# Sliding-window layer of a four-layer decoder step: the prompt's attention and the samples' attention put into one phase

## What is computed

```python
SWA_GROUPS = ((128, 1), (512, 4), (2048, 16))     # window and dilation, 4 heads each, head size 64
q, k, v = jnp.split(h @ w_qkv, 3, axis=-1)        # q and k are then normalised per head
# prompt: every query sees the last win/dil keys at distance dil
s = einsum('bcnihd,bcnjhd->bcnhij', qb, kk) * HEAD_DIM ** -0.5 + bias   # masked outside the window
# samples: past rows come from cache_swa_kv0/1/2 (128, 512, 1024 rows kept), new rows are appended
s = einsum('bthd,btnhd->bthn', q, kg) * HEAD_DIM ** -0.5 + bias_tab[rel_bucket(n * dil)].T
lse = logsumexp(s); p = exp(s - lse); o = einsum('bthn,btnhd->bthd', p, vg)
# the three groups are weighted by the softmax of their lse, then  o @ w_out
# outputs too: the new caches (old rows shifted, new rows stored at the end)
```

## Time and profile before

| | |
|---|---|
| median of 3 runs | 2106.91 us (2106.85 to 2110.78) |
| profiled execution, its own time | 2107.75 us |
| its span, first to last instruction | 2106.1 us |
| TensorE matmul busy | 1934.6 us, 92% |
| VectorE, ScalarE, GpSimd busy | 1186.1, 960.5, 478.6 us |
| mean granted TensorE clock | 0.953 |

### The profile page before, as it was taken

How to read it: one execution, slowest core, us unless ns; L and a number is a source line. 1 busy time by engine, 2 the same in 40 slices (tenths; PEclk the granted TensorE clock), 3 DMA queues, 4 the chain that set the end, 5 groups by cost and what they waited for, 6 DMA issues and landing times. The chain is left out here.

```text
span 2106.1 us, 37643 instructions
## 1 busy us (share of the span) xinstructions
PE 1934.6 (92%) x14726; PEld 1830.9 (87%) x14726; DVE 1186.1 (56%) x2046; ACT 960.5 (46%) x1566; POOL 478.6 (23%) x480
## 2 busy tenths in 40 slices
PE   6899979999998678999997887999998999799999
PEld 4899969999997457999996666999988999699998
DVE  4677764555443235554445775555466777555543
ACT  3666663444342124443343554444347666434432
POOL 3222212333100002442102321333112222023420
PEclk9999989999998688999999998999999999899999
DMA  6367755555552094655656742665563667456554
GB/s 181 98 203 235 235 173 161 160 163 147 172 170 79 17 275 122 169 161 144 176 192 206 288 170 76 176 169 152 164 191 113 221 218 222 135 154 166 161 150 133
DMA packets 502033, 352.63 MB, mean 167 GB/s; under 512 B 14154, under 2 KB 487100, under 8 KB 501084
## 3 DMA queue, kind: packets, MB, share of 16 engines
q1 hardware_dynamic: 495156, 306.03, 49.9%
q0 software_dynamic: 6272, 43.92, 5.5%
q10 hardware_dynamic: 430, 0.29, 0.1%
HBM read 326.58 MB, written 50.63 MB: 179 GB/s over the span
## 5 line engine op out<-in xcount | busy, mean ns | idle before, releaser
L268 PE MATMUL ps<-xh,whi 128*128 128x288 f32 x2368 | 657.8, 304 | 10.0 <-PEq L176 9.9
L268 PE MATMUL ps<-xl,whi 128*128 128x288 f32 x2368 | 647.1, 300 | 0.0
L240 DVE TENSOR_TENSOR wlo<-raw,whi 128x2048 fp32r<-128x2048 f32 (+3 forms) x241 | 501.8, 2083 | 245.2 <-ACT whi L229 245.0
L229 ACT ACTIVATE whi<-raw 128x2048 fp32r<-128x2048 f32 (+3 forms) x241 | 419.1, 1740 | 263.5 <-PE ps L276 231.4
L268 PEld LDWEIGHTS ps<-xh,whi 128*128 128x128 f32 x2368 | 454.7, 192 | 12.2 <-issue 10.5
L268 PEld LDWEIGHTS ps<-xl,whi 128*128 128x128 f32 x2368 | 455.4, 192 | 0.8
L276 PE MATMUL ps<-xh,wlo 128*128 128x288 f32 x2368 | 354.6, 300 | 0.0
L276 PEld LDWEIGHTS ps<-xh,wlo 128*128 128x128 f32 x2368 | 328.8, 190 | 1.1
L520 POOL TENSOR_TENSOR gh<-sg,ut 128x288 f32<-128x288 f32 x88 | 216.3, 2458 | 353.0 <-ACT sg L461 353.0
L268 PE MATMUL ps<-hh,whi 128*128 128x288 f32 x704 | 189.7, 296 | 0.0
L268 PE MATMUL ps<-hl,whi 128*128 128x288 f32 x704 | 189.6, 297 | 0.0
(11 more groups left out here) (319 smaller groups left out, 2702.4 us busy)
## 6 DMA issues: line engine op xcount, KB each, us to landing
raw<-in_ffn_w_in SPq DMA_DIRECT2D x176, 512.0 KB, 5.0
raw<-in_ssm_w_in SPq DMA_DIRECT2D x80, 512.0 KB, 4.8
raw<-in_ffn_w_out SPq DMA_DIRECT2D x64, 384.0 KB, 4.0
raw<-in_ffn_w_out SPq DMA_DIRECT2D x64, 320.0 KB, 3.2
H<-in_state_ssm SPq DMA_DIRECT2D x32, 512.0 KB, 7.6
out_ssm_sample<-H SPq DMA_DIRECT2D x32, 512.0 KB, 6.5
raw<-in_ssm_w_out SPq DMA_DIRECT2D x32, 512.0 KB, 5.0
Kp_L<-in_cache_diff_k SPq DMA_DIRECT2D x64, 256.0 KB, 4.5
```

The lines of the kernel that those rows point to most:

```text
L229: act.activation(wts["hi"][:, s, 0:width], raw[:, s, 0:width], ACT.Copy).then_inc(hi_ready.sem, 1)
L240: dve.tensor_tensor(wts["lo"][:, s, 0:width], raw[:, s, 0:width], wts["hi"][:, s, 0:width].bitcast(F32), ALU.subtract).then_inc(lo_ready.s ...
L268: pe.matmul(out, W[0][:, kk, j, :], x_[:, k, :], stop=False, start=(part == 0 and kk == 0 and x_ is seg.hi), skip_group_check=True)
```

## The change

It removes the phase boundary inside layer 1's attention and writes the eight prompt units between the samples' instructions, on every engine. In words:

- `load_keys` is passed to `project`: the first round's keys (16 loads) go out on SyncE's queue in two halves, during and after the weight blocks. The wait on the page table moves into layer 2's own function.
- Keys are turned in two parts: 8 pieces of the wide cache (4 transposes each), then 8 pieces of the other two caches (3 transposes each), into one buffer `KT` that both parts use. Scores are made after each part.
- The second round's keys load into the same buffers as they come free; its values wait for the end of the first round's values (`pv_done`), since `V1`, `V0`, `V2` are used by both rounds.
- Turned pieces go round three PSUM banks, prompt scores have a place of their own (banks 3 and 4), the samples' scores and values share banks 5 and 6, the prompt's results are in bank 7.
- The prompt's bias and maximum are one VectorE instruction (`tensor_tensor_reduce`) instead of two.
- The new rows' 29 stores go out on GpSimd's queue instead of SyncE's. Behind them GpSimd copies the new keys' bias (`new_bias`), which the samples' maximum waits for.

```diff
-                        sp.wait_ge(table_in.sem, table_in.at(1))
...
+        def load_keys(sp, half):
+            for j in (2 * half, 2 * half + 1):
+                load_wide(sp, j, 0, K1[:, j, :, :], key_in[j])
+                load_rest(sp, j, 0, K0[:, j, :], K2[:, j, :, :], key_in[j])
...
-                Linear(4, 6, 2, columns(A["swa_w_out"][0], 6, 2)))
+                Linear(4, 6, 2, columns(A["swa_w_out"][0], 6, 2)), load_keys=load_keys)
...
+                for t in range(T):
+                    sp.dma_start(rb[32 * t:32 * t + 32, :], A["rel_bias"]).then_inc(loaded.sem, loaded.inc())
+                sp.dma_start(barred, A["barred_swa"]).then_inc(loaded.sem, loaded.inc())
+                sp.dma_start(oh, A["onehot_swa"]).then_inc(loaded.sem, loaded.inc())
...
+                for j in range(J):
+                    load_wide(sp, j, 1, V1[:, j, :, :], val_in)
+                    load_rest(sp, j, 1, V0[:, j, :], V2[:, j, :, :], val_in)
+                for j in range(J):
+                    sp.wait_ge(piece_turned.sem, piece_turned.at(at["key", 0, 2 * j + 1] + 1))
+                    load_wide(sp, J + j, 0, K1[:, j, :, :], key_in[j])
...
+                sp.wait_ge(pv_done.sem, pv_done.at(1))
+                for j in range(J):
+                    load_wide(sp, J + j, 1, V1[:, j, :, :], val_in)
+                    load_rest(sp, J + j, 1, V0[:, j, :], V2[:, j, :, :], val_in)
+                sp.wait_ge(copied.sem, copied.at(29))
...
-                        sp.dma_start(out[rows], KV[:, t, :, cols]).then_inc(stored.sem, stored.inc())
+                        pool.dma_start(out[rows], KV[:, t, :, cols]).then_inc(copied.sem, copied.inc())
...
+                for q in range(R):
+                    pool.wait_ge(laid.sem, laid.at(9 + NB))
+                    if q:
+                        pool.wait_ge(mx_ready.sem, mx_ready.at(q))
+                    pool.tensor_copy(bias[:, N_OLD:], BN[:, q, :]).then_inc(new_bias.sem, new_bias.inc())
...
+                unit_scores(0)
+                turn(0, 0, 0, 3)
+                unit_scores(1)
+                turn(0, 0, 3, 6)
+                tables_()
+                unit_scores(2)
+                turn(0, 0, 6, 8)
+                unit_turn(0)
+                scores_wide(0)
+                unit_values(0)
...
+                values(0)
+                unit_turn(5)
+                unit_values(5)
+                unit_scores(7)
+                scores_wide(1)
+                turn(1, 1, 0, 8)
+                scores_rest(1)
+                turn_out(0)
+                unit_turn(6)
+                unit_values(6)
+                unit_turn(7)
+                unit_values(7)
+                turn_probs(1)
+                values(1)
+                turn_out(1)
...
+                    dve.tensor_tensor_reduce(
+                        Su[:, r, :, 0:n], flat[:, 3 * 512:3 * 512 + 768].rearrange("p (g n) -> p g n", g=3)[:, :, 0:n],
+                        BT.rearrange("p h t k -> p h (t k)")[:, hh::4, 2 * P - n:2 * P], -1.0, 3.0e38,
+                        ALU.add, ALU.min, su[:, r, 0:1]).then_inc(u_lowest.sem, u_lowest.inc())
...
+                unit_lowest(0)
+                keys(0, 0, 0, 3)
+                lay_queries()
+                lay_tables()
+                unit_lowest(1)
+                unit_scale(0)
```

More of the change, by code:

```diff
@@ L1963, in swa @@
[L1963 to L1983 removed]
+            R = 2
@@ L2104, in swa @@
             at = {piece: n for n, piece in enumerate(order)}
-            mover = [0 if kind == "prob" and p == 0 else 1 if kind != "key" else p % 2 for kind, _, p in order]
+            mover = [0 if kind == "turned" else 1 if kind == "out" else p % 2 for kind, _, p in order]
             count = [sum(e == mover[n] for e in mover[:n + 1]) for n in range(len(order))]
-            def last_piece(j):
-                return (2 * N_OLD * (j + 1) - 1) // 512
             def wait_moved(eng, *piece):
@@ L2145, in _ @@
[L2145 to L2147 removed]
+                        val_in.sem, val_in.inc())
+                for j in range(J):
[4 more added lines that the diff above has]
+                    load_wide(sp, J + j, 0, K1[:, j, :, :], key_in[j])
@@ new lines, in tables_ @@
+                def tables_():
+                    pe.wait_ge(laid.sem, laid.at(8))
+                    pe.wait_ge(loaded.sem, loaded.at(T + 2))
+                    for g, lo, n in KEYS + tuple((g, N_OLD + g * T, T) for g in range(3)):
+                        out = ps[:, 7, lo - N_OLD:lo - N_OLD + n] if lo >= N_OLD else flat[:, 2560 + lo:2560 + lo + n]
+                        pe.matmul(out, LT[:, g, :], oh[:, lo:lo + n], start=True, stop=False)
+                        mm = pe.matmul(out, barred[:, N_OLD + 12:], barred[:, lo:lo + n], start=False, stop=True)
+                    mm.then_inc(tables.sem, tables.inc())
@@ L2230, in _ @@
-                pe.wait_ge(laid.sem, laid.at(4))
-                pe.wait_ge(loaded.sem, loaded.at(T + 2))
-                for g, lo, n in KEYS + tuple((g, N_OLD + g * T, T) for g in range(3)):
-                    new = lo >= N_OLD
-                    out = ps[:, 6, lo - N_OLD:lo - N_OLD + n] if new else flat[:, 2048 + lo:2048 + lo + n]
-                    pe.matmul(out, LT[:, g, :], oh[:, lo:lo + n], start=True, stop=False)
-                    mm = pe.matmul(out, barred[:, N_OLD + 12:], barred[:, lo:lo + n], start=False, stop=True)
@@ new lines, in unit_turn @@
+                def unit_turn(u):
+                    qt, hh, n, rows, r = unit(u)
+                    pe.wait_ge(u_summed.sem, u_summed.at(2 * u + 2))
+                    tiles = [(g, kt) for g in range(3) for kt in range(qt + 1)]
+                    for p in range(qt + 1):
+                        m = at["turned", u, p]
+                        wait_moved(pe, *order[m - 3])
+                        for k, (g, kt) in enumerate(tiles[3 * p:3 * p + 3]):
+                            mm = pe.matmul(ps[:, m % 3, k * P:(k + 1) * P], Su[:, r, g, kt * P:(kt + 1) * P], DR[:, r, :],
+                                           start=True, stop=True)
+                        mm.then_inc(piece_turned.sem, piece_turned.inc())
@@ new lines, in keys, with unit_exp @@
+                def keys(q, part, lo, hi):
+                    for i in range(lo, hi):
+                        if i % 2 == 0:
+                            move(act, copy, "key", q, 8 * part + i)
+                def unit_exp(u):
+                    qt, hh, n, rows, r = unit(u)
+                    act.wait_ge(u_lowest.sem, u_lowest.at(u + 1))
+                    act.activation(Su[:, r, :, 0:n], Su[:, r, :, 0:n], ACT.Exp, scale=-1.0, bias=su[:, r, 0:1],
+                                   accum_out=su[:, r, 1:2]).then_inc(u_weighed.sem, u_weighed.inc())
@@ L2293, in _ @@
+                unit_move(4)
+                unit_exp(5)
+                keys(1, 0, 4, 8)
+                move(act, copy, "prob", 0, 0)
+                unit_exp(6)
+                unit_move(5)
+                unit_exp(7)
+                keys(1, 1, 0, 8)
+                unit_move(6)
+                exp_sample(1)
+                unit_move(7)
+                move(act, copy, "prob", 1, 0)
             @block.vector
@@ L2371, in swa @@
+                unit_out(5)
+                unit_lowest(7)
+                unit_scale(6)
+                keys(1, 1, 0, 8)
+                lowest_of(1)
+                out(0)
+                unit_scale(7)
+                unit_out(6)
+                unit_out(7)
+                move(dve, copy, "prob", 1, 1)
+                stage_out(1)
+                out(1)
+        memB.close()
         mem.close()
```

595 lines of the change are left out of this document (293 added, 302 removed).

## The result

The changed kernel takes 2059.51 us (median of four runs, 2056.42 to 2063.7); the kernel before takes 2108.85 beside it (2106.85 to 2113.36). The ratio is 0.9761, with a 95% interval of 0.9736 to 0.9785: faster by 2.4%. The profiled execution of the changed kernel has a time of 2056.42 us, a span of 2054.8 and a mean granted clock of 0.971.

A forecast was written before the change was run, and what follows sets the result against it. Bound: layer 1 attention's serial chain at the low clock. Terms 6.6 + 10.9 + 1.5 + 56.0 + 11.4 = 86.4 us against 135.8, 49.4 less: 2107.75 - 49.4 = 2058.4, forecast 2058 us, range 2044 to 2074.

The forecast's parts named there:

- The bound and the cure: Layer 1's attention: a serial chain at the low clock bounds it; weaving cuts the phase from 135.8 to 86.4 us.
- the range of 75 to 80: Sign that the forecast is right: TensorE busy 75 to 80 us of a stretch of about 86 us.
- Start: Phase's beginning: the tables wait 6.6 us for small loads, with TensorE busy 3.8 us of that.
- Tables: TensorE's bias table matmuls after the start: 10.85 us at 1.2 GHz, as in the kernel before.
- The end of 5.4: Lower end for the table matmuls: 5.4 us, if they run at 2.4 GHz.
- Slow rest: Behind the tables: 1.5 us added for about 3 us of other work at 1.2 GHz.
- Middle: Woven units and samples: 48.7 us of TensorE work at layer 2's 87% busy share, 56.0 us.
- Tail: After the last unit: second round's probabilities, values, staging and output, the same chain as before, 11.4 us.
- Loads: Keys moved into the projection cost 0, at most 5.2 us; second round's values hidden with 5.8 us to spare.
- Stores: 29 issues on GpSimd, 0.58 us each, 16.8 us, done 20 us in; cost 0.
- The rule of the Trainium skill: VectorE shuts GpSimd out: a 620 ns DMA takes 3100; an estimated 90 us before the copy behind the stores.
- The fused maximum: Prompt units on VectorE: saves about 1 us per large unit from a chain that no longer decides; counted 0.

The follow-up runs named there:

- unwoven kernel: Changed kernel with loads, stores, fused maximum and buffers kept, but all eight prompt units before the samples' work on every engine: 2106.65 us.
- The early loads: Changed kernel with the tables' operands (`rb`, `barred`, `oh`) loaded in the projection, into memory that outlasts the phase: 2055.55 us.
- the filler: Changed kernel plus seven dummy 128x256 matmuls on TensorE in the wait ahead of the bias tables: 2058.62 us.
- two-step kernel: Changed kernel with the prompt units' addition and maximum as two VectorE instructions again: 2073.27 us, and 2064.63 us (0.9777 of before) when run again.
- filled kernel: The two-step kernel plus five dummy 128x256 matmuls ahead of the third prompt unit's turning: 2067.39 us, 0.9794 of before.

## Why the prediction was right, step by step

**The bound and the cure held.** The unwoven kernel keeps the old length with everything else changed, so the serial chain at the low clock was the bound, and interleaving removes it (131.7 against 88.7). Stretch 88.7 against 86.4; TensorE busy 76.2 of it, in the range of 75 to 80; no wait for a DMA.

**Start: 8.2 us, priced 6.6.** The bound was right, small loads before the tables, but I took their time from a phase that begins with an idle SyncE. The `rb` issue alone is 3.02 us here and was 1.98 before. The early loads show the rest: with the small loads gone from the phase's head, TensorE is at the tables 4.5 us in.

**Tables: 10.85 us, priced 10.85 to the last digit.** That is in part luck. The gap ahead of them did lower the clock, but the filler shows that this reason was not the whole of it: without the gap they would still have cost 8.1. The end of 5.4 that I kept for the range is not reached even with the gap gone and the operands there (6.2), since the clock doubles but these matmuls don't take half: the two entries of one with 4 columns take 0.39 us at the whole clock and 0.59 at the low one.

**Slow rest: 6 us of work at half clock, 3 us, priced 1.5.**

**Middle: 60.1 us, priced 56.0 (57.5 with the slow rest).** The share of busy time was a good loan from layer 2: 90% against 87%. What was too small is the work. 54.2 us were recorded, 51.2 without the slow rest, against 48.7. The keys' transposes are the main part of that, and the fault is in how the prediction read its row. The 1.51 us for 14 transposes in the earlier trace rows is a row of weight loads (PEld). TensorE's own rows of the kernel before, of 56 and of 14 transposes, are

```profile
753.08 7.69 PE L2171 MATMUL ps<-cst,K 128*128 128x128 f32 x56
...
769.87 1.75 PE L2171 MATMUL ps<-cst,K 128*128 128x128 f32 x14 [1.00 <-DMA K<-in_cache_swa_kv]
```

All 112 are busy for 14.8 us there, 0.132 each, and not the 12.1 of the prediction. In the changed kernel they are busy for 15.6 us, of which 0.9 is the slow rest: 0.131 each. So cutting the pieces from 14 a round to 16 changed neither their number nor their price; the 0.108 was the price of the loads. In the middle stand 88 of the 112: 11.6 us at the whole clock where the prediction had 9.5, which is 2.1 of the 2.5 us.

**Tail: 9.6 us, priced 11.4.** It is the same chain. In the kernel before the clock had fallen once more in it, which the prediction took over without seeing it: a window there, in the second round's values, reads

```profile
791.00:792.00 1.00, 1.00 (x16) 0.69 (x12) 0.00 (x0) 0.00 (x0) 0.00 (x0) 0.50 0.00 0
```

The first 32 matmuls of the values took 3.50 us then and take 1.93 now, at clock 1.00. That is 1.6 of the 1.8.

**Loads.** The values of the second round are issued from 720.16 to 729.84, 9.7 us in place of 11.17, and nothing waits. The keys' early loads were right at 0 for the projection. What my text had wrong is their cover: "a block would come late by at most 5.2 us" priced the loads against the projection; taken out of it they cost the woven phase 12.2.

**Stores.** 29 in 17.2 us, priced 16.8, 0.59 each. The rule of the Trainium skill that I weighed ("SBUF — State Buffer", "A bandwidth-pool intuition that's wrong (but worth ruling out)") would have had 3.1 us for some of them. No row here shows that: the three groups of eight took 4.65, 4.76 and 5.03. VectorE was busy only 2.08 of the 10.8 us in which most were issued, so this is a light test of the rule.

**The fused maximum: counted at 0, worth about 4 us of the middle (3.8 and 4.9 in two executions).** This term was wrong, and not only its size. I argued that a chain that no longer decides can't give anything. VectorE's list also holds the moves of keys' pieces: put off by 1 us they lengthen TensorE's wait at the third unit from 1.20 to 2.18 us and add two waits further on, and the longer wait brings the clock down again. By the filled kernel the waits are the larger part, 2.7 us, and the clock 1.1 to 2.2. The sum did not suffer only because it never used the term: the middle was priced by layer 2's share of busy time, whatever the maximum costs.

Summed, the start is 1.6 us over its price, the middle with the slow rest 2.6 (1.5 by the slow rest, 2.5 by the work, less 1.4 of waits), the tail 1.8 under: 2.4, which is 88.7 against 86.4 but for rounding. The time, 2058 against 2059.51, came out closer than its terms deserved, and that is luck: the errors of start and middle and that of the tail have opposite signs, and the phase also began 1.4 us earlier than in the profiled execution of before, which the change did not do.

## What to carry to other kernels

A serial chain costs twice on TensorE, by its waits and by the lower clock that they bring: here 17 and 26 of the 43 us between the unwoven and the woven kernel. Interleave it with work that is independent, and load that work's first operands in the stage before, or the weave starts with a wait for them (12 us here, and 8 more for the tables' small operands). An edit on an engine that is "never the bound" is at nothing only if its list holds nothing that the bound waits for; look up what is queued behind it, and what the bound does in the wait that it lengthens (here from 1.20 to 2.18 us). And price TensorE's work by TensorE's rows, not by those of its weight loads (1.51 and 1.75 us for the same 14 transposes).

## What the runs showed of the hardware

- The granted clock fell to 0.50 while TensorE's records show it busy in every microsecond: in the tables with the gap filled (window from 679), in the tables with early operands (from 674), and in the tables with the keys in the phase (from 692). The tables are matmuls of up to 512 columns whose stationary part has 128 rows and 4 rows in turn, and at their end some of 4 columns. With the gap filled the fall came at 679.3, before the first matmul of 4 columns (681.16), so those were not needed for it. The Trainium skill's page "TensorE: Matmul & The Clock Gate", in its Part 1, says that the clock follows how busy the array has been. The filled wait of the two-step kernel agrees (1.00 with the filler, 0.50 without). The tables don't by the busy share of the records; whether the small stationary part is the reason was not tried.
- How long the clock stays low varies widely: 17 us in the changed kernel from 670, 10 with the filler, under 7 with early tables, and 7 and 3 at the same second fall of one kernel. TensorE was busy nearly all of each.
- The same four `rb` loads were issued in 1.90 to 3.28 us, depending on the kernel and the execution: 3.02 and 2.70 in the changed kernel's two.
- An idle time of 1.20 us at the third unit left the clock at 1.00 in both executions of the changed kernel (and in those with stores on SyncE, the filler or early tables); 2.18 us there brought it to 0.50 in both of the two-step kernel.
